# Mixture-of-experts stage of a streaming encoder step: gathering tokens for eight experts at once, and adding the expert outputs in the scatter

## The reference

```python
scores = sigmoid(t @ w_router); choice = scores + b_router
# 4 of 8 groups, then 8 of 64 experts per token: idx, w (288 x 8)
for each chosen (token, expert):
    y[token] += w * ((silu(t[token] @ w_gate[e]) * (t[token] @ w_up[e])) @ w_down[e])
shared = (silu(t @ w_sh_gate) * (t @ w_sh_up)) @ w_sh_down
x = x + gt2 * (y + shared);  out = rms_norm(x, g_final)
```

## Time and profile before

| | us |
|---|---|
| median of 3 runs | 929.48 (927.88 to 931.46) |
| the profiled execution, its own time | 932.22 |
| its span in the trace | 930.4 |
| TensorE busy | 860.4 (92%) |
| VectorE, ScalarE, GpSimd busy | 268.6, 247.9, 88.4 |
| transfers | 273.84 MB, 294 GB/s over the span |
| share of TensorE in the chain that ended last | 85% |

### The profile page before, as it was taken

The page is one execution under the profiler, slowest core; times in us unless marked ns, Lnnn a source line. Parts: engine busy times, 40 slices in busy tenths (PEclk is TensorE's granted clock), DMA queues, the critical chain, the costliest instruction groups (busy, mean ns, idle before and its releaser), DMA issues.

```text
span 930.4 us, 13928 instructions
## 1 busy us (share of the span) xinstructions
PE 860.4 (92%) x4436; PEld 470.1 (51%) x4437; DVE 268.6 (29%) x797; ACT 247.9 (27%) x484; POOL 88.4 (10%) x189
## 2 busy tenths in 40 slices
PE   7699999797898999999999999999999999999962
PEld 3199983534686744444444444444444444444521
DVE  2354426435226611111211121121212112121118
ACT  2353424134113312131222212121222213121231
POOL 3000011200022000101101010101101010100000
PEclk9889989798798999999999999999999999999977
DMA  8934447452526369099995999699996999999183
GB/s 326 362 133 160 182 181 276 151 181 92 222 81 263 103 272 376 40 366 415 428 425 245 406 427 426 271 371 420 427 425 254 397 427 426 426 427 426 77 302 157
DMA packets 55370, 273.84 MB, mean 294 GB/s; under 512 B 12720, under 2 KB 13056, under 8 KB 27312
## 3 DMA queue, kind: packets, MB, share of 16 engines
q1 hardware_dynamic: 42064, 258.23, 68.3%
q0 software_dynamic: 6560, 12.55, 3.6%
q10 hardware_dynamic: 6720, 2.70, 1.1%
HBM read 261.34 MB, written 22.07 MB: 305 GB/s over the span
## 4 chain that ended last, share of the span: by engine, by line
PE 85%; DVE 5%; DMA 4%; ACTq 2%; issue 2%; ACT 1%; SPq 0%; POOL 0%; POOLq 0%; DVEq 0%
PE psum L1174 27%; PE psum L1193 13%; PE psum L1150 10%; PE psum L870 8%; PE psum L1157 4%; PE psum L1071 4%; DMA expert_w<-in_w_exp_down 3%; PE psum L840 3%; PE psum L1099 2%; PE psum L1166 2%; PE psum L1089 1%; ACTq L480 1%; PE psum L1183 1%; PE psum L1226 1%; PE psum L825 1%
## 5 line engine op out<-in xcount | busy, mean ns | idle before, releaser
L1174 PE MATMUL psum<-expert_w,xg 128*64 128x512 f32 x1184 | 263.9, 598 | 3.4 <-DMA expert_w<-in_w_exp_down 1.7
L1174 PEld LDWEIGHTS psum<-expert_w,xg 128*64 128x64 f32 x1184 | 85.8, 137 | 150.1 <-issue 149.4
L1193 PE MATMUL psum<-expert_w,hidT 128*64 128x512 f32 x592 | 135.2, 599 | 0.0
L1150 PE MATMUL psum<-h2hl,sel 128*128 128x512 f32 x380 | 97.8, 403 | 0.5 <-ACT acc L616 0.5
L1150 PEld LDWEIGHTS psum<-h2hl,sel 128*128 128x128 f32 x380 | 68.4, 188 | 43.7 <-issue 30.0
L634 ACT ACTIVATE silg<-psum 128x256 f32<-128x256 f32 x37 | 14.2, 384 | 260.9 <-PE psum L1174 260.9
L1193 PEld LDWEIGHTS psum<-expert_w,hidT 128*64 128x64 f32 x592 | 39.3, 137 | 69.6 <-issue 69.6
L1597 DVE SCALAR_TENSOR_TENSOR hid<-psum,ws,silg 128x256 f32<-128x256 f32 x37 | 17.9, 483 | 195.7 <-ACT silg L634 195.7
L623 ACT COPY xs<-psum 128x512 f32<-128x512 f32 x76 | 44.5, 586 | 58.1 <-PE psum L1150 58.1
L1607 DVE COPY y_slot<-psum 128x512 f32<-128x512 f32 x37 | 25.6, 691 | 117.7 <-PE psum L1193 117.7
L1157 PE MATMUL psum<-ident,xs 128*128 128x128 f32 x304 | 47.7, 280 | 0.5 <-ACT xs L623 0.2
(11 more groups left out here) (370 smaller groups left out, 846.5 us busy)
## 6 DMA issues: line engine op xcount, KB each, us to landing
expert_w<-in_w_exp_gate SPq DMA_DIRECT2D x64, 1024.0 KB, 9.9
expert_w<-in_w_exp_up SPq DMA_DIRECT2D x64, 1024.0 KB, 11.9
expert_w<-in_w_exp_down SPq DMA_DIRECT2D x64, 1024.0 KB, 12.7
ring<-in_w_ada SPq DMA_DIRECT2D x24, 1024.0 KB, 7.0
pair<-in_w_in SPq DMA_DIRECT2D x6, 2048.0 KB, 9.6
y_rank<-y_d SPq DMA_DIRECT2D x8, 1024.0 KB, 12.9
pair<-in_w_out SPq DMA_DIRECT2D x2, 2048.0 KB, 8.2
x_tok<-in_x_prompt SPq DMA_DIRECT2D x2, 512.0 KB, 4.1
```

The source lines that it names most:

```text
L1150: last = mm(bank[q][:, :], sel[:, t // 2, :, :], h2hl[:, t, 4 * q:4 * q + 4, :], start=t == 0, stop=t == 4)
L1174: last = mm(bank[3][CAP * x:CAP * x + CAP, :].rearrange("p (g n) -> p g n", g=2), xg[:, k, CAP * x:CAP * x + CAP], expert_w[2 * u + x][:, ...
L1193: last = mm(bank[4 + half][CAP * x:CAP * x + CAP, :], hidT[:, i, CAP * x:CAP * x + CAP], expert_w[2 * u + x][:, 2, o:o + 512], start=i == ...
```

## The change

1. **Gather.** Four pairs (eight experts) form a quad. `sel4` holds the slots of a quad's eight experts, 512 columns. One *token chunk* loads 128 columns of the tokens as weights and streams `sel4`: five products give the tokens of all eight experts for 128 of the 1024 model dimensions, already with the model dimension on partitions. Each last block of a pair computes two chunks for the next quad, so four pairs make eight. The transposes L1157 and one of ScalarE's two copies are left out there. There are two buffers `xgT`, laid over tiles no longer in use. Further blocks keep the old gather with its transposes. Before the loop all eight chunks of the first quad are computed.
2. **Slots.** The weights and target rows of a pair (`ws`, `row_f`) are computed one quad ahead.
3. **Scatter.** `y_d` has two rows per token, one for each half of the slots. The scatter adds to them (`compute_op=ALU.add`). GpSimd clears `y_d` with a transfer of zeros during the input projection.
4. **Tail.** Only two rows per token are read back, 2.4 MB; TensorE's sums are left out. VectorE has three instructions per group of tokens and one scaling. `gt2B` is loaded by SyncE after the loop, into the place of `h2hl`.
5. **Front.** The small loads go to GpSimd's queue. VectorE makes two of the four copies of `ada_row`. The first piece of `w_in` comes as two transfers.
6. The loops' bodies now hold eight pairs instead of two.

```diff
+        def token_chunk(k):
+            for t in range(5):
+                last = mm(bank[k % 2][:, :], h2hl[:, t, k, :], sel4[:, t // 2, :, :, :], start=t == 0, stop=t == 4)
+            last.then_inc(s["xs_ps"], 1)
+
+        def slots(chosen, p):
             for i in range(3):
-                last = mm(bank[2][:, 0:8], sel[:, i, :, :], wp[:, i, :, :], start=i == 0, stop=i == 2)
-            last.then_inc(s["slots_ps"], 1)
+                last = mm(bank[2][:, 8 * p:8 * p + 8], chosen[:, i, :, :], wp[:, p, i, :, :], start=i == 0, stop=i == 2)
+            return last
...
             last.then_inc(s["pgu_ps"], 1)
-            gather(n + 1, 0)
-            gather(n + 1, 1)
+            pe.wait_ge(s["sel_ok"], num(pe, n + 2))
+            pe.wait_ge(s["ws_ok"], num(pe, n + 1))
+            if last_of_pair:
+                if p == 0:
+                    pe.wait_ge(s["sel4_ok"], num(pe, quad + 2))
+                slots(sel4[:, :, p, :, :], p).then_inc(s["slots_ps"], 1)
+                token_chunk(2 * p)
+            else:
+                slots(sel, p).then_inc(s["slots_ps"], 1)
+                gather(0)
+                gather(1)
             pe.wait_ge(s["hid_ok"], num(pe, n + 1))
...
-            gather_T(n + 1, 0)
-            gather_T(n + 1, 1)
+            if last_of_pair:
+                token_chunk(2 * p + 1)
+            else:
+                gather_T(e, 0)
+                gather_T(e, 1)
...
             pool.indirect_dma_start(y_d[:, :], bass.IndirectOffsetOnAxis(ap=row[:, 0:1], axis=0), y_slot[:, :], None,
-                                    bounds_check=TOPK * N - 1, oob_is_err=False).then_inc(s["y_out"], 16)
+                                    bounds_check=2 * N - 1, oob_is_err=False, compute_op=ALU.add).then_inc(s["y_out"], 16)
...
+            dve.wait_ge(s["row_ok"], num(dve, n + 2))
+            slot_values((c + QUAD) % (2 * QUAD) if last_of_pair else c, p).then_inc(s["ws_ok"], 1)
             dve.wait_ge(s["yl_ps"], num(dve, n + 1))
             dve.tensor_copy(y_slot[:, 0:512], bank[4][:, :]).then_inc(s["y_dve"], 1)
+            if last_of_pair and p == QUAD - 1:
+                select_quad(b + (QUAD + 1), num(dve, n * 2 + (KC + 2)))
...
+            dve.wait_ge(halves_in(i)[0], halves_in(i)[1] + 16)
+            link(dve.tensor_tensor(y[0:n, 0, :], y[0:n, 0, :], y[0:n, 1, :], ALU.add))
+            link(dve.tensor_tensor(y[0:n, 0, :], y[0:n, 0, :], gt2B[0:n, 1 if i == 2 else 0, :], ALU.mult))
+            dve.tensor_tensor(y[0:n, 0, :], y[0:n, 0, :], base_tok[0:n, i, :], ALU.add).then_inc(s["y_sum"], 1)
...
+            if n == FIRST_WIN:
+                for q in range(2):
+                    sp.dma_start(dst[:, :, 256 * q:256 * q + 256], src[:, :, 256 * q:256 * q + 256]).then_inc(ring_in[slots_of[n][q]], 16)
...
-            for j in range(4):
+            for j in range(4 if r else 2):
                 act.copy(ada_row[32 * j:32 * j + 2, :], bank[b][32 * j:32 * j + 2, :]).then_inc(s["ada_row"], 1)
...
+        pool.dma_start(y_d.rearrange("(p a) d -> p (a d)", a=9).rearrange("p (r n) -> p r n", n=768), nothing[0:64, :].unsqueeze(1).broadcast_to([64, 12, 768])).then_inc(s["y_clear"], 16)
```

More of the change, by code:

```diff
@@ L100, in layer @@
     scT = sb("scT", [P, KC, 2])
+    XT = place["at"]
     xT = sb("xT", [P, KC, N])
@@ L220, in layer @@
     g_finB = sb("g_finB", [P, D])
-    four = sb("four", [P, NS_])
     ssqT = sb("ssqT", [P, 3])
@@ L272, in layer @@
         loads[sl[0]] += 1
+        if n == KC:
+            loads[sl[1]] += 1
         turn.append(loads[sl[0]])
@@ L285, in piece @@
         return ring[slots_of[n][0]] if pieces[n][1] == 1 else pair[slots_of[n][0] // 2]
+    second_turn = 1 + sum(1 for n in range(FIRST_WIN) if slots_of[n][0] == slots_of[FIRST_WIN][1])
     SHARED = FRONT
@@ L436, in _ @@
             for u in range(2):
-                further, first = pair_blocks(sp, it * 2 + (u - 2))
+                further, earlier, first = pair_blocks(sp, it * 2 + (u - 2))
                 done = sp.snap(first + further + 1)
@@ L641, in act_block @@
             act.copy(y_slot[:, 512:D], bank[5][:, :]).then_inc(s["y_act"], 1)
-        slots_in(0)
-        gathered(0)
-        with act.Fori(0, PAIRS // 2) as it:
-            for u in range(2):
-                each_block(act, it * 2 + u, lambda n, j, last: act_block(n))
+        for k in range(KC):
+            act.wait_ge(s["xs_ps"], k + 1)
+            act.copy(xgT[0][k // 4][:, k % 4, :], bank[k % 2][:, :]).then_inc(s["xg_ok" if k == KC - 1 else "xs_ok"], 1)
+        act.wait_ge(s["fin_ok"], KC)
+        with act.Fori(0, PAIRS // (2 * QUAD)) as it:
+            for m in range(2 * QUAD):
+                g, p, b = m // QUAD, m % QUAD, it * (2 * QUAD) + m
+                each_block(act, b, lambda n, e, j, last: act_block(n, e, g, p, last))
         for i in range(3):
@@ L689, in _ @@
         pool.wait_ge(s["consts"], 1)
+        pool.memset(ada_row[:, :], 0.0).then_inc(s["row_zeros"], 1)
+        pool.wait_ge(s["row_zeros"], 1)
+        with nc.allow_non_contiguous_dma(reason="vectors of a few hundred elements"):
+            for dst, src in small[3:]:
+                pool.dma_start(dst, src).then_inc(s["small_in"], 16)
+            pool.dma_start(pastf[:, :, :], cache_fox_logf[0, 0].rearrange("(j p) h -> p j h", p=P)).then_inc(s["state_in"], 16)
+        for c in range(2):
+            pool.dma_start(states[:, 4, c, :], state_gla[0, 0, 2 * c:2 * c + 2].rearrange("h k v -> (h k) v")).then_inc(s["state_in"], 16)
         pool.memset(qA[FD:FD + 2, :, :], 1.0).then_inc(s["ones_ok"], 1)
@@ L1144, in _, with gather @@
         pe.wait_ge(s["table_ok"], 1)
[L1146 to L1148 removed]
+        def gather(q):
             for t in range(5):
@@ new lines, in slot_values, with dve_block @@
+        def slot_values(c, p):
+            for x in range(2):
+                half = slice(CAP * x, CAP * x + CAP)
+                dve.tensor_reduce(ws[half, c:c + 1], bank[2][half, 8 * p + x:8 * p + 4:2], AX, ALU.add)
+                last = dve.tensor_reduce(row_f[half, c:c + 1], bank[2][half, 8 * p + 4 + x:8 * p + 8:2], AX, ALU.add)
+            return last
+        def dve_block(n, b, g, p, j, last_of_pair):
+            c = QUAD * g + p
+            chosen = experts_of(b + QUAD if last_of_pair else b)
+            at = None if last_of_pair else dve.snap((j + 1) * CAP)
+            dve.wait_ge(s["xs_ps"], num(dve, n * 2 + KC))
+            if not last_of_pair:
+                select_further(chosen, at)
+            weights_of(chosen, p).then_inc(s["sel_ok"], 1)
@@ L1595, in dve_block @@
             dve.wait_ge(s["sl_ok"], num(dve, n + 1))
             dve.wait_ge(s["ws_ok"], num(dve, n + 1))
-            dve.scalar_tensor_tensor(out=hid[:, :], in0=bank[3][:, DE:2 * DE], scalar=ws[:, 0:1], in1=silg[:, :],
+            dve.scalar_tensor_tensor(out=hid[:, :], in0=bank[3][:, DE:2 * DE], scalar=ws[:, c:c + 1], in1=silg[:, :],
                                      op0=ALU.mult, op1=ALU.mult).then_inc(s["hid_ok"], 1)
             dve.wait_ge(s["y_gone"], num(dve, n + 1))
-            for x in range(2):
-                p = slice(CAP * x, CAP * x + CAP)
-                last = dve.tensor_reduce(row_f[p, :], bank[2][p, 4 + x:8:2], AX, ALU.add)
@@ L1613, in _ @@
+        for p in range(QUAD):
+            last = weights_of(experts_of(p), p)
+        last.then_inc(s["sel_ok"], 1)
         for k in range(KC):
```

261 lines of the change are left out of this document (132 added, 129 removed).

## The result

The changed kernel takes 947.9 us (median of 4 runs, 947.5 to 950.1) against 930.5 for the kernel before measured beside it: ratio 1.0181 (1.0158 to 1.0203). It is slower, by 17 us. The forecast was 911 us with a range of 892 to 934, so time and sign are both wrong. The profiled execution took 947.49 us, its span is 945.4 us.

What follows compares the result with a forecast made beforehand. It took TensorE to set the rhythm only because of further blocks, with weight transfers binding elsewhere. 932.2 - 4.8 - 11.1 + 17.0 - 20.0 = 913.3 us, less 2.7 for profiling: 910.6, said as 911; range 892 to 934.

Steps and rivals of the forecast that it cites:

- Front, -4.8: Before the input projection: without small loads and with two copies on ScalarE, `hhi` starts at 38.1, saving 4.8 us.
- Tail, -20.0: After the last block: less read-back and no TensorE sums cut the tail from 48.0 to 28.0 us.
- The add, +17.0: Adding scatter: one more reading, 0.68 us a block, counted in 25 transfer-bound pairs, +17.0 us (0 to +34).
- B: Rival on the scatter: the add costs 1.36 us a block, giving 928 us; chance 0.11.
- A: Rival on the scatter: the add is free as reads overlap with writes, giving 894 us; chance 0.26.
- C: Rival: the scatter's landing grows and becomes the bound, deciding from 13.8 us, giving 955 us; chance 0.12.
- The loop, -11.1: Loop over experts: lighter last blocks, mostly hidden by waits for weights, end it 11.1 us earlier (-7 to -15).
- The term for five pairs: Loop, after a further block: transfers need 80.2 us for five pairs, less 1.3 for an earlier request, so 78.9.
- The entry: Before the loop: the first quad's eight chunks make the first gate/up end 5.4 us late (3.5 to 8).
- Code, +0: Loop bodies of eight pairs: the forecast's sum held no cost for fetching code again.
- Rival D: Long loop's three jumps back fetch code again, 0 to 21 us, say 10, giving 921 us; chance 0.08.
- E: Rival in the loop: TensorE stays the bound through stalls, blocks keep 14.86 us, at least 910 us; chance 0.05.

Runs made afterwards that it cites:

- e11: Kernel before with the adding scatter, light tail and new front, keeping old gather and two-pair loops: 926.5 us, ratio 0.9953.
- e3: Changed kernel with its loops over pairs written out, so no jumps back: 936.7 us, ratio 1.0050 to the kernel before.
- e12: Kernel before with the new front alone: 927.2 us, ratio 0.9950.
- e8: Changed kernel with loops written out and the scatter writing plainly instead of adding: 917.2 us, ratio 0.9840 to the kernel before.
- e2: Changed kernel with the scatter writing plainly instead of adding, bodies of eight pairs kept: 932.7 us, ratio 1.0015 to the kernel before.
- e15: Kernel before with five of the ten gather products left out in each last block of a pair: 924.4 us, ratio 0.9929.
- e9: Kernel before with all loops written out: 934.3 us, ratio 1.0034.
- e10: Kernel before with the adding scatter and light tail, and its loops written out: 930.6 us, ratio 0.9990.
- e4: Kernel before with the adding scatter and light tail, keeping old gather, old front and two-pair loops: 930.7 us, ratio 0.9979.
- e5: Kernel before with bodies of eight pairs in TensorE's loop alone: 950.3 us, ratio 1.0205.
- e6: Kernel before with bodies of eight pairs in VectorE's loop alone: 944.5 us, ratio 1.0143.

## Why the prediction was wrong

In medians the change goes 931 (before), 926.5 (add, tail, front: e11), 936.7 (new gather, written out: e3), 947.9 (bodies of eight pairs). By the steps of the forecast:

- **Front, -4.8.** Right: `hhi` at 38.09 (37.2 to 39.3 in the traces of e12, e11, e3 and e8, which have the same front), and 4.0 us less in e12.
- **Tail, -20.0.** Right within 1 us: 29.0 us for 28.0.
- **The add, +17.0.** Right within 3 us: 19.5 (e3 against e8), 15.2 (the changed kernel against e2), and 3.3 to 3.9 us in each five pairs of the table above (e3 against e8), 0.66 to 0.78 a pair. The scatters' queue has 7.8% of the engines' time in e3 and 4.8% in e8; 0.078 x 934.6 - 0.048 x 917.8 = 28.8 us over 37 scatters is 0.78 us each for the 0.68 taken, and so is 19.5 us over 25 pairs. "One more reading" was nearly it, and B's 1.36 was far. The estimate of 0.58 that was worked out from the Trainium skill, "DMA: Bandwidth & Descriptors", section "Anatomy of one DMA", is a quarter below the trace's 0.78. A (the add is free) and C (its landing becomes the bound) are out: the landing went from 7.8 to a median of 9.5 us, at most 10.8, under the 13.8 from which it decides.
- **The loop, -11.1.** The first failed step. What the forecast called -11.1, with no add and no jump, is about +9: e8 is 13.7 us below its kernel before, and while front and tail alone give 4.0 and 19. The failure has three parts.
  - *The term for five pairs*, the largest: "five pairs cost 80.2, less 1.3 because pair 5's gate is asked for after 13.6 instead of 14.86 us", so 78.9. From an idle start to the start of the fifth pair's products it was 80.7 to 81.1 us in e15 and 81.9 to 82.6 in e8. The 80.2 took the median of two landings for the later one; it was 1.1 us short of the 81.3 at that very place, and 2.2 short of the 82.4 at pair 8. And the credit of 1.3 came only in part: in the last three stretches e15, with requests 1.1 us earlier, needs 0.7 us less than the kernel before, in the first 1.3. The 15.6 us for each pair at the end hold: from the last landing for pair 26 to that for pair 31 pass 78.0 us before and 77.9 in e15. Over the loop the term is worth 16.5 - 7.3 = 9 us, by e15.
  - *The entry.* Pair 2's gate was asked for at 338.2, 1.1 us later than forecast (336.48 - 4.8 + 5.4 = 337.1), and at 340.6 in e8, 3.5 later. A part stood there ahead of the entry: from the start of the 32 products before the chunks (L1089 before, L1120 after) to that issue pass 25.3 us in the kernel before, 31.3 in the changed one and 32.2 in e3 and e8. So the entry costs 6.0 and 6.9 us for the 5.4.
  - *The rest of the loop.* The stretches of e8 are 1.1, 1.3 and 3.0 us above those of e15. Of this 0.9 to 1.6 are a longer need of the transfers. In the last one 1.5 more are TensorE's clock: the first block of pair 20 has its gate and up in 8.78 us instead of 7.09, and as it is a further block, no wait for weights follows that would hide it. The same block takes 8.65 us in e3. VectorE's eight selections matter little in e8: TensorE waits 1.2 and 1.0 us for them, and waits for weights follow both times (0.4 and 2.5 us).
- **Code, +0.** The second failed step. Rival D had the mechanism, the three places and the size ("0 to 21, say 10": 11.2 by e3, 15.5 by e2 against e8, 19.5 in the kernel before), but a chance of 0.08 and no place in the sum. The forecast itself counted about 2140 instructions beside the limit of 2048 that the Trainium skill states ("Runtime: NRT & Kernel Launch", "Instruction fetch mechanics"); what spoke against D, that today's loop fetches nothing, speaks of a body of a quarter of the length. E said that the blocks would keep their 14.86 us; they came down to 13.5 and waited for weights instead, so it has the time of the loop nearly right by another cause.

No single step gives a slower kernel. With D's 11 the forecast would have been 922; with the loop at +9 instead of -11 it would have been 931; with both it is 942, and with the front's 0.8, the add's 2.5 and the tail's 1 it is 946. The other 1 to 2 us aren't accounted for. (The limit for a scatter's landing should read 15.6 - 1.7 = 13.9; nothing hangs on it.)

What stays open: why e8 needs 0.9 to 1.6 us more than e15 for its five pairs. The stream of code may be it: e9 needs 0.3 to 1.8 us more than the kernel before, but e10 only 0.4 to 0.5 more than e4, and no run takes the stream out of e8. The later entry with written-out loops is seen but not explained either: of the 2.4 us between the changed kernel and e8 at pair 2, 1.5 stand already ahead of the chunks, and in the rest the second four chunks take 6.45 us instead of 4.83, at a granted clock of 0.73 instead of 1.00. Bodies of four pairs with the new gather weren't tried, since its two buffers alternate every four pairs and their places stand fixed in a body of eight.

## What to carry to other kernels

Before work is taken off an engine, look at what the other resource needs for the same stretch: here TensorE's 104 us shrank to 103 when 1.1 us was taken from every last block, and two blocks that already came 0.15 and 0.37 us late said so. Take the need from an idle start to a landing in the same place of the loop, and to the last of the landings that the products wait for, not to the median of several. And don't count an earlier request in full while the queue still holds work: it gave 0.7 to 1.3 us here. Count the instructions of a loop body before it is lengthened: the profile's instruction queues tell at once (q8 and q14, 17 and 9 packets or 56 and 36) whether the code is fetched again, and then a jump back costs 4 to 10 us with the transfer engines full.

## What the runs showed of the hardware

- A loop body either stays in an engine or is fetched as a whole in each iteration. Between 350 and 885 us the kernel before has no instruction packet at all, the changed kernel 38 on q8 and 26 on q14, one on q8 for each 14 us. With the body of eight pairs e5 has 40 on q8 there, and e9, which has all 32 pairs written out one after the other, 36.
- A jump back outside what is held costs each engine several fetches one after another. In e6 VectorE is idle from 626.4 to 636.7 us, and the windows 628 to 632, 632 to 636 and 636 to 640 hold one packet of q14 each, those from 620 to 628 none.
- The stream itself is cheap where it runs ahead in order: 3.2 us (1.2 to 5.0) in e9, nothing in e10.
- The granted clock of TensorE was lower behind some waits for weights and not behind others of the same length. The further block of pair 20 in e8, at a granted clock of 0.81 (688.9 to 697.8 us), where the same block of pair 14 ran at 1.00 (584.5 to 591.7 us) behind a wait of 2.34:

```profile
688.95 8.78 PE L1212 MATMUL psum<-expert_w,xgT 128*64 128x512 f32 x32 [2.33 <-DMA expert_w<-in_w_exp_down]
```

- A scatter that adds costs GpSimd more too: 1.55 us per issue (1542 to 1731 ns) against 0.98 for a plain write in e8 (medians).
- The 16 transfer engines don't run dry together, and with the add they drift further apart. The rate in 40 slices of 12 us from 488 us in the kernel before, then of 10 us from 484 us in e4, each where a further block lets the transfers end:

```profile
GB/s 437 410 382 410 410 328 328 246 218 218 191 164 164 137 55 27 27 0 0 0 0 0 0 0 0 0 232 410 423 423 260 0 0 0 0 0 0 0 0 0
```

```profile
GB/s 459 426 459 360 328 360 393 328 328 295 229 295 295 262 262 262 229 229 197 262 197 98 164 131 164 131 98 98 66 66 0 0 0 0 0 0 0 0 0 0
```

From 410 GB/s to nothing it takes 3.6 us (slices of 0.3) before and 6.9 us (slices of 0.25) with the add. At other such places it takes 3.9 and 2.7 us before and 6.9 in e4; e8 and e3, which differ in the add alone, take 4.2 to 4.5 and 6.0. If products wait for the slowest engine's part, some of the add's price is this drift. That wasn't tried by itself.
